# Order of the probability transposes in a soft-attention pipeline: before a unit's scores, three units behind

## The reference, cut to what matters

```python
# differential attention: 4 heads, 2 maps each, key width 32, value width 64
s = einsum('bhmqd,bhmkd->bhmqk', qi, k) * scale
p = masked_softmax(s, t[:, None] >= pos[None, :])
a = p[:, :, 0] - lam * p[:, :, 1]
o = einsum('bhqk,bhkd->bhqd', a, v)          # then a norm per head

# sparse attention: 8 heads in 2 groups, width 64, three branches with gates
o = g[..., 0:1] * o_cmp + g[..., 1:2] * o_slc + g[..., 2:3] * o_win
```

## Time and profile before

| what | value |
|---|---|
| median of 3 runs | 3843.06 us |
| lowest and highest | 3836.14 and 3843.15 us |
| span of the profiled execution | 3839.6 us |
| PE busy over the span | 3501.5 us (91%) |
| DVE busy | 2121.2 us (55%) |
| ACT busy | 1218.9 us (32%) |
| soft attention, layer 0 | about 577 to 712 us |
| soft attention, layer 1 | about 1665 to 1800 us |
| granted PE clock, whole span | 0.962 |

### The profile page before, as it was taken

How to read it: one execution, slowest core, us unless ns; L and a number is a source line. 1 busy time by engine, 2 the same in 40 slices (tenths; PEclk the granted TensorE clock), 3 DMA queues, 4 the chain that set the end, 5 groups by cost and what they waited for, 6 DMA issues and landing times. The chain is left out here.

```text
span 3839.6 us, 41511 instructions
## 1 busy us (share of the span) xinstructions
PE 3501.5 (91%) x14092; PEld 2382.7 (62%) x14092; DVE 2121.2 (55%) x4268; ACT 1218.9 (32%) x2239; POOL 1608.2 (42%) x957
## 2 busy tenths in 40 slices
PE   8999999999999999999999999897787778788777
PEld 6888686688888887766888876663333333333333
DVE  5536257433326454466333065488777777666665
ACT  3332226443333323155333233432212222212222
POOL 2446430244455456211444533345544444444542
PEclk9999999999999999999999999998988989998899
DMA  6536320122435355200233321369999999999997
GB/s 247 184 105 256 118 99 1 45 99 96 167 130 197 137 202 188 94 17 23 88 98 99 104 78 56 113 247 418 421 421 422 421 421 422 421 422 421 422 420 314
DMA packets 140415, 830.67 MB, mean 216 GB/s; under 512 B 15713, under 2 KB 16353, under 8 KB 63841
## 3 DMA queue, kind: packets, MB, share of 16 engines
q0 software_dynamic: 73728, 536.90, 33.8%
q1 hardware_dynamic: 66528, 291.77, 21.5%
HBM read 826.52 MB, written 2.10 MB: 216 GB/s over the span
## 5 line engine op out<-in xcount | busy, mean ns | idle before, releaser
L277 POOL TENSOR_TENSOR wlo<-wraw,whi 128x1024 fp32r<-128x1024 f32 x357 | 904.4, 2538 | 1479.3 <-ACT whi L273 1478.9
L273 ACT ACTIVATE whi<-wraw 128x1024 fp32r<-128x1024 f32 x357 | 377.6, 1058 | 649.5 <-DMA wraw<-in_wts 365.8
L284 PE MATMUL f_ps<-f_hh,whi 128*128 128x512 f32 x1408 | 549.5, 390 | 1.7 <-DVE f_hl L405 1.7
L286 PE MATMUL f_ps<-f_hh,wlo 128*128 128x512 f32 x1408 | 547.9, 389 | 0.0
L285 PE MATMUL f_ps<-f_hl,whi 128*128 128x512 f32 x1408 | 547.9, 389 | 0.0
L2036 PE MATMUL g_psF<-g_low,g_diagb 128*128 128x512 f32 x660 | 326.7, 647 | 96.0 <-ACT g_diagb L2096 96.0
L2036 PE MATMUL g_psF<-g_own,g_diagb 128*128 128x512 f32 x576 | 289.4, 654 | 68.4 <-ACT g_diagb L2096 68.4
L578 DVE TENSOR_TENSOR f_a<-f_sg,f_ps 128x512 f32<-128x512 f32 x88 | 60.5, 688 | 511.7 <-PE f_ps L286 497.1
L2036 PE MATMUL g_psF<-g_top,g_diagb 128*128 128x512 f32 x524 | 260.9, 648 | 70.9 <-ACT g_diagb L2096 70.8
L2090 ACT ACTIVATE g_dotb<-g_dotb 128x4 f32<-128x4 f32 (+2 forms) x146 | 29.9, 205 | 891.4 <-DVE g_dotb L2183 891.4
L2036 PEld LDWEIGHTS g_psF<-g_low,g_diagb 128*128 128x128 f32 x660 | 133.9, 208 | 285.4 <-issue 285.4
(11 more groups left out here) (413 smaller groups left out, 6394.2 us busy)
## 6 DMA issues: line engine op xcount, KB each, us to landing
wraw<-in_wts SPq DMA_DIRECT2D x359, 512.0 KB, 3.7
m_wrow<-in_ada SPq DMA_DIRECT2D x44, 1024.0 KB, 7.3
m_erow<-in_ada SPq DMA_DIRECT2D x28, 1024.0 KB, 5.2
p_wt<-in_wtok SPq DMA_DIRECT2D x2, 3168.0 KB, 10.3
p_wt<-in_w SPq DMA_DIRECT2D x2, 3072.0 KB, 9.7
g_low<-in_uv,idx POOLq DMA_INDIRECT x165, 24.8
g_own<-in_uv,idx POOLq DMA_INDIRECT x144, 24.3
g_top<-in_uv,idx POOLq DMA_INDIRECT x131, 24.8
```

The lines of the kernel that those rows point to most:

```text
L273: self.nc.scalar.activation(self.T.whi[:, j % 4], self.T.wraw[:, j % 2], ACT.Copy).then_inc(self.M["w_hi"], 1)
L277: self.nc.gpsimd.tensor_tensor(self.T.wlo[:, j % 4], self.T.wraw[:, j % 2], self.T.whi[:, j % 4].bitcast(F32), ALU.subtract).then_inc(self ...
L284: self.nc.tensor.matmul(out, hi, xh, start=first, stop=False)
L286: return self.nc.tensor.matmul(out, lo, xh, start=False, stop=last)
```

## The change

The distance between a unit's scores and its transposes becomes a constant, LAG = 3. On PE the transposes of unit g - 3 stand at the head of iteration g, ahead of the scores of unit g; they stood behind them, for unit g - 2. The V of a pair moves from the even iterations to the odd ones. On ACT the copy K is that of unit g - 3 instead of g - 2. On DVE `out` moves from u = 3 to u = 4. No instruction is added or removed, and no buffer changes.

```diff
-    SLOTS = 4
+    SLOTS, LAG = 4, 3
@@ tensor
-                for g in range(G + 3):
+                for g in range(G + LAG + 2):
                     t, u = g // U - DA_TILES, g % U
                     nsa = 0 <= t < NSA_TILES
+                    if LAG <= g < G + LAG:
+                        turn_probs(g - LAG)
                     if g < G:
                         scores(g)
                     if g < len(FILL):
...
                         da_spread(t - 1)
                     if nsa and u == 3:
                         cmp_scores(t)
-                    if 2 <= g < G + 2:
-                        turn_probs(g - 2)
                     if t == 0 and u == 5:
                         da_sums()
                     if nsa and u == 7:
                         cmp_turn(t)
-                    if g >= 4 and g % 2 == 0:
-                        values((g - 4) // 2)
+                    if g >= LAG + 2 and (g - LAG) % 2 == 0:
+                        values((g - LAG - 2) // 2)
@@ scalar
-                for g in range(G + 2):
+                for g in range(G + LAG):
...
-                    if g >= 2:
-                        take_turned(g - 2)
+                    if g >= LAG:
+                        take_turned(g - LAG)
                     if g < G:
                         exps(g)
@@ vector
-                    if u == 3 and g >= U:
+                    if u == 4 and g >= U:
                         out(g // U - 1)
```

## The result

| | before | after |
|---|---|---|
| median, us | 3840.73 (3836.14 to 3843.15) | 3883.19 (3877.31 to 3884.36) |
| ratio to before, 95% interval | | 1.0111 [1.0098, 1.0124] |
| span of the profiled execution, us | 3839.6 | 3880.3 |
| soft attention, layer 0 and layer 1, us | 134.3, 133.9 | 152.8, 153.2 |

The change makes the kernel slower by 42.5 us. The median of before is 3840.73 and no longer 3843.06, as a fourth execution has come in. A stage here runs from its first scores to the products that nobody reads behind its last V. The two stages grew by 18.5 and 19.3 us, together 37.9 of the 40.7 us between the spans.

The account below looks back on a forecast made before the run. PE's order was taken as the bound in soft attention, with DVE close behind. Terms 0.6 + 5.2 + 3.7 + 2.4 + 1.8 = 13.7 us per layer, 27.4 for two, gave 3870 us; range 3847 to 3884.

Parts of the forecast that it names:

- rival 3: The clock also falls in the three NSA tiles after the first, both layers, about 2 us each: 3882 us; chance 0.17.
- The gain: On PE, V fills the gaps before T; a steady tile's stalls of 1.09 and about 0.9 us go.
- the main cost: Steady NSA tile: T3 waits 2.3 us for K2, then `cmp_turn` holds PE 1.7 us; tile +2.4 us.
- rival 1: The lead pays: ACT's exps no longer wait for T, K leaves PE's path; up to 21 us faster, 3822; chance 0.11.
- the first cause: NSA tile: T3 waits 2.3 us because K2, which empties `psT`, is queued on ACT behind the compressed exp.
- the second to third S4: Interval between these NSA tiles: 2.4 us as in a steady tile plus 1.25 for the `da_out` wait, +3.7 us.
- the third to fourth: Interval between these NSA tiles' S4: the steady tile's loss, +2.4 us.
- the end: Last NSA tile to stage end: +2.4 less what T6 and the last V give back, taken as +1.8 us.
- The first to second S4: First NSA tile: later square, V0 and T3 at low clock, `cmp_turn` wait, table load, `da_out` wait; +5.2 us.
- The DA part: No new wait of T; later `out` costs about what the moved V takes away: +0.6 us, bounds -2 and +2.
- the clock: The fall before `da_sums` stays, counted as before; new NSA waits could bring falls, priced 2 us each, outside the sum.
- Rival 2: PE's order hardly changes, each new wait replaces an old one, within 7 us either way: 3843 us; chance 0.10.

Follow-up runs that it names:

- E8: Changed kernel with the compressed keys' chain (scores, maxima, exp) earlier, as far as PE's new order allows, and `out` back at u = 3: 3850.69 us.
- E1: Changed kernel with ACT's loop as before, K(g-2); PE's new order and `out` at u = 4 stay: 3873.29 us.
- E6: Changed kernel with `cmp_turn` and `da_sums` moved later on PE, behind V and the next T, as before the change: 3878.34 us.
- E10: Changed kernel with two products that nobody reads on PE ahead of T3 in each NSA tile and two ahead of `da_sums`: 3870.68 us.
- E12: Repeat run of the kernel before with the compressed keys' chain earlier in the first NSA tile only: 3835.79 us.
- E11: Kernel before with the compressed keys' chain (scores, maxima, exp) earlier in the first NSA tile only: 3837.15 us.

## Why the prediction was right, and by how much it was short

The forecast said slower, 3870 us, in a range of 3847 to 3884. Measured: 3883.19, inside, at the upper end; 42.5 us where 27.4 were summed. Of the 15.1 us that were missing, 10.5 lie in the stages (37.9 against 27.4), 2.8 in the rest of the profiled execution and 1.8 between the profiled executions and the medians. That the sum came out low and the range still held owes something to its upper end having been set by rival 3.

**The gain** came as said: T's waits for DVE went from 10.4 to 3.2 us. So did **the main cost**. T3 was to start 5.6 us after S4, S6 at 6.2, T4 at 7.4, S7 at 8.2, `cmp_turn` at 11.1 and the next S0 at 13.5. In the second tile of layer 0, where the clock stayed up, they start at 5.7, 6.35, 7.5, 8.3, 11.3 and 13.7. T3 waits 2.20 us (forecast 2.3), `cmp_turn` 1.66 (1.7). The Trainium skill, "Perfetto Trace Analysis", section "Optimization Strategy", says to make the dependency start sooner that ends the gaps; by it rival 1 was put up, which fell. It was no clean test of the rule: the gaps went, yet W3 started 2.65 us after S4 (656.76 - 654.11), not sooner than the 2.05 of before (672.80 - 670.75); T only came later in PE's order. The same section says that a repeating gap can mean too little PSUM. The 8.0 us of T waiting for `psT` look like it; but E8 has 2.5 us left with the same PSUM, and no run here gave T more.

**What the forecast called the first cause is one of several that stand in for each other.** E1 takes T3's wait away and leaves 35.6 us; E6 takes `cmp_turn`'s away and leaves 39.5; only E8, which gets the chain out of the way at more than one place, brings back 31. The forecast added the waits of one tile in sequence, which came out for the sum, and says nothing on what removing one would bring.

**The terms.** `cmp_scores` waited 0.86 and 1.14 us for `da_out` (forecast 1.25). At full clock the second to third S4 grew by 4.2 (forecast 3.7), the third to fourth by 2.9 (2.4) and the end by 2.4 (1.8): each about 0.5 short. In the steady tile of E10's layer 1, S0 comes 13.7 us after S4 (13.5), and the way to the next S4 takes 10.9 (10.4), as not the whole 0.9 before T6 came back. (The forecast's own 13.5 + 10.4 is 23.9 and not 24.0.) The first to second S4 grew by 6.6 in both layers (5.2). It is the term that was most undersized. `cmp_turn` waited 1.6 and 2.2 us there (about 1.3), and T6 waited 0.8 us for K5, which stands on ACT behind a second table load of 1.28 us, the one that brings exp back; the forecast had one such load, at 0.4. These two hold 0.6 to 1.3 of the missing 1.4 us. The DA part grew by 0.1 (0.6). Together the terms make 32.2 us for two layers, where 27.4 were summed. The second load and T6, in layer 0 of the changed kernel:

```profile
638.20 1.28 ACT L1141 ACT_TABLE_LOAD   x1 [0.20 <-DVE a_nm L1189]
```

```profile
641.47 1.06 PE L1046 MATMUL a_psT<-const,a_p 128*128 128x128 f32 x8 [0.79 <-ACT a_pt L1153]
```

**The step that failed is the clock**, beside that term. The forecast counted the fall before `da_sums` "as before", and kept falls in the NSA tiles for rival 3, with a chance of 0.17. The first part held as far as it counts. The wait before `da_sums` came out as forecast (3.25 us, forecast some 3.5). The slow stretch behind it lasted 10.2 us instead of 6.8 in layer 0 and 6.8 as before in layer 1, and the interval grew by 6.6 us in both. So the clock doesn't explain what that term lacks. The second part failed: falls came in two tiles of three in layer 0 and in all three in layer 1, and cost the 5.7 us worked out under E10. Third to fourth S4 in layer 0 had 6.8 us of low clock and lost 1.4 us by it. There the slow work partly takes the place of a wait: `cmp_turn` waited only 0.30 us in that tile, instead of 1.66.

```profile
687.71 2.08 PE L1031 MATMUL a_psS<-z 64*128 64x512 f32 x4
689.90 1.49 PE L1046 MATMUL a_psT<-const,a_p 128*128 128x128 f32 x6
691.32 1.82 PE L1031 MATMUL a_psS<-z 64*128 64x512 f32 x4
693.65 0.63 PE L1086 MATMUL psN<-const,a_cs 128*64 128x128 f32 x4 [0.30 <-DVE a_cs L1234]
```

The same scores and transposes took 1.13 and 0.82 us in the tile before. So what happened is the forecast's sum, 4.8 us larger, and rival 3 in five of its six tiles, at 1.1 us for each instead of 2. That the median stands about 1 us from rival 3's 3882 is luck: that rival's sum is 27.4 + 12, and the stages show 32.2 + 5.7.

**Rival 2** (each new wait takes only the place of an old one) is refuted by the idle time: 10.5 us became 20.3 in layer 0. **Rival 1** needed K2 done within 3.3 us of S4; it starts 5.2 us behind S4 (659.34 - 654.11), as forecast.

## What to carry to other kernels

A step taken a unit later on one engine is not free for the engine that reuses its buffer: before lengthening a lead, write down who empties the buffer, what is queued in front of that copy, and on which engine that in turn waits. Here two PSUM halves hold one unit, so the copy had no unit to spare, and the steps that were put ahead of the transposes stopped all that is behind them. Look for the slow step in front of that copy before giving up the order: moving it took away most of the loss (E8). And where PE gains a wait of about 2 us per tile, price the lower clock behind it too; it was about a seventh of what the stages lost here.

## What the runs showed of the hardware

- The same wait does not always bring the clock down. In layer 0 T3 waited 2.20 us in the second tile and 2.19 in the third and the last. The clock stayed at 1.00 through the second tile and fell in the other two; in layer 1 the three waits were 2.20 us each, and it fell every time. In the second and the third tile PE's instructions ahead of the wait are the same.
- 3.4 us at the lower clock cost a tile 0.7 to 1.4 us and not half of them, 1.7, as the tiles with and without a fall show (E10 against the changed kernel). In one of them `cmp_turn` waited 0.30 us instead of 1.66, so slow work takes the place of a wait.
- With products that nobody reads in T3's wait no fall followed it in any of six tiles (E10), and the tile that had no fall anyway kept its 26.84 us, although the waits themselves don't end sooner. The two stages together became 2.9 us shorter.
- Code that an edit doesn't touch varies by several microseconds with the clock. The stretch from the last product of V to the first L2036 that reads `g_low` took 814.0 us with 20.0 us of low clock (before), 813.4 with 22.8 (E10), 818.0 with 30.0 (after), 817.9 with 32.8 (E12), 818.7 with 36.2 (E11) and 821.4 with 37.1 (E1): roughly half a microsecond for each of low clock. So a difference of less than some 5 us between two medians here is not to be credited to a stage unless the profile shows it there. That holds for E11, for most of E10's and E6's gain, and for the last 4 us of the 35.6 of E1. Whether time saved in a stage brings such falls about is open.
